# Attention's product with the values: values stationary and two query tiles moving, in place of probabilities stationary and values moving

## What is computed

```python
# q, k: (B, S, 4 heads, 2, 64); v: (B, S, 4 heads, 128)
scores = einsum("bqhmd,bkhmd->bhmqk", q * 64**-0.5, k)      # causal
p = softmax(scores, axis=-1)
a = p[:, :, 0] - lam * p[:, :, 1]
o = einsum("bhqk,bkhe->bqhe", a, v)                          # 128 dimensions per head
o = o * rsqrt(mean(o * o, axis=-1) + 1e-5) * subln_g * (1 - lam_init)
y_b = (o.reshape(b, s, 512) * silu(b_z)) @ w_b_out
```

## Time and profile before

| | us |
|---|---|
| median of 3 runs | 2308.67 (2306.83 to 2308.70) |
| the profiled execution | 2308.06 |
| its span, first to last instruction | 2306.3 |
| PE busy | 2278.6 (99%) |
| DVE busy | 1482.0 (64%) |
| ACT busy | 748.6 (32%) |
| POOL busy | 258.7 (11%) |

### The profile page before, as it was taken

How to read it: one execution, slowest core, us unless ns; L and a number is a source line. 1 busy time by engine, 2 the same in 40 slices (tenths; PEclk the granted TensorE clock), 3 DMA queues, 4 the chain that set the end, 5 groups by cost and what they waited for, 6 DMA issues and landing times.

```text
span 2306.3 us, 30415 instructions
## 1 busy us (share of the span) xinstructions
PE 2278.6 (99%) x11248; PEld 1860.0 (81%) x11248; DVE 1482.0 (64%) x3042; ACT 748.6 (32%) x1690; POOL 258.7 (11%) x250
## 2 busy tenths in 40 slices
PE   7999999999999999999999999999999999999998
PEld 6888888878888888888788888888878787888886
DVE  4787867773666665564567667665456666587752
ACT  4333332332333331121344344102135454441021
POOL 3455400100000000010000000001000000000010
PEclk9999999999999999999999999999999999999999
DMA  8877788887555545576644454556664444435555
GB/s 312 275 274 273 269 295 289 289 324 289 187 174 176 182 163 186 198 259 240 239 175 174 163 184 145 183 188 243 253 239 163 152 161 154 155 116 188 191 192 201
DMA packets 90610, 490.84 MB, mean 213 GB/s; under 512 B 9312, under 2 KB 9568, under 8 KB 45408
## 3 DMA queue, kind: packets, MB, share of 16 engines
q1 hardware_dynamic: 90464, 488.90, 59.6%
HBM read 375.61 MB, written 113.25 MB: 212 GB/s over the span
## 4 chain that ended last, share of the span: by engine, by line
PE 95%; DVE 2%; DMA 1%; ACT 1%; issue 1%; SPq 0%; DVEq 0%; ACTq 0%
PE PJ L637 73%; PE SC L696 6%; PE OB L758 5%; PE SC L728 5%; PE TB L737 3%; PE OB L696 1%; PE PJ L696 1%; DMA PX<-x_t 0%; PE TB L764 0%; DMA UC<-x 0%; PE TB L771 0%; DVE ZA L1253 0%; PE SC L637 0%; DVE Wp L1169 0%; PE OB L637 0%
## 5 line engine op out<-in xcount | busy, mean ns | idle before, releaser
L637 PE MATMUL PJ<-hT,Wp 128*128 128x512 f32 x6480 | 1575.6, 395 | 0.5 <-DVE PX L1448 0.5
L637 PEld LDWEIGHTS PJ<-hT,Wp 128*128 128x128 f32 x6480 | 1186.6, 188 | 254.1 <-issue 17.0
L1369 DVE SCALAR_TENSOR_TENSOR ACCS<-UA,col,ACCS 128x512 f32<-128x512 f32 x464 | 358.1, 812 | 0.1
L916 ACT ACTIVATE PX<-SC,negm 128x512 f32<-128x512 f32 (+3 forms) x320 | 196.3, 622 | 93.7 <-DVE negm L1208 73.1
L936 ACT ACTIVATE ZA<-TB 128x512 fp32r<-128x512 f32 (+3 forms) x160 | 85.6, 535 | 394.7 <-PE TB L737 394.6
L1253 DVE TENSOR_TENSOR ZA<-TB,ZA 128x512 fp32r<-128x512 f32 (+3 forms) x160 | 97.6, 610 | 178.4 <-ACT ZA L936 177.6
L1208 DVE TENSOR_REDUCE negm<-SC 128x2 f32<-128x1024 f32 (+3 forms) x160 | 169.2, 1060 | 35.3 <-PE SC L728 33.1
L970 ACT ACTIVATE TG<-PJ,col 128x512 f32<-128x512 f32 x64 | 44.1, 689 | 358.3 <-PE PJ L637 358.3
L758 PEld LDWEIGHTS OB<-VM,ZA 128*128 128x128 f32 x1088 | 145.4, 189 | 11.2
L758 PE MATMUL OB<-VM,ZA 128*128 128x128 f32 (+1 forms) x1088 | 154.1, 281 | 0.0
L696 PE MATMUL SC<-Wp,KM 128*128 128x512 f32 x384 | 121.4, 389 | 0.0
(11 more groups left out here) (172 smaller groups left out, 2016.0 us busy)
## 6 DMA issues: line engine op xcount, KB each, us to landing
Wp<-split_weights SPq DMA_DIRECT2D x264, 1024.0 KB, 4.8
split_weights<-Wp SPq DMA_DIRECT2D x88, 1024.0 KB, 4.9
Wraw<-w_stream SPq DMA_DIRECT2D x88, 512.0 KB, 5.8
KM<-keys SPq DMA_DIRECT2D x24, 512.0 KB, 4.5
VM<-values SPq DMA_DIRECT2D x24, 512.0 KB, 4.2
PX<-x SPq DMA_DIRECT2D x16, 512.0 KB, 6.8
out<-PX SPq DMA_DIRECT2D x16, 512.0 KB, 10.9
keys<-KM SPq DMA_DIRECT2D x12, 512.0 KB, 5.8
```

What stands on the lines that cost most here:

```text
L637: mm = pe.matmul(pj(c, r)[:, :], wt, rhs[:, 1 if q == 1 else 0, k, :], start=(n == 0), stop=(n == 3 * ktiles - 1))
L916: a = act.activation(PX[:, t % 2, j, m, 0:w], SC[k][:, m, 0:w], ACT.Exp, bias=negm[:, t % 2, j, m:m + 1], accum_out=lsum[:, t % 2, j, m:m ...
L1369: a = dve.scalar_tensor_tensor(out=acc, in0=src, scalar=col[:, n:n + 1], in1=acc, op0=ALU.mult, op1=ALU.add)
```

## The change

**Product with the values.** The values are stationary (v_hi and v_lo, 128x128 each), and the turned probabilities move, 256 columns wide: two query tiles 2q and 2q+1 side by side, a **pair** q. The output stands in `OB` with the head's dimensions on partitions and 256 queries in columns. A **turn** (q, j, g) takes two key blocks of a pair, that is four 128x128 transposes (three at the diagonal) into `TB`, and is followed by six products. There are 144 turns; all are 256 wide save three products in each of the 32 turns in which a block of one tile is masked away, which are 128 wide. The turns of a pair begin when its second tile is done, `TURN_GAP` steps apart (8, 6, 4, 3 for the four chunks).

**Norm.** The 32 pairs take the place of 64 tiles. ACT copies `OB` out (`o_copy`), DVE clamps a copy, ACT squares all of it, PE multiplies the squares by a 128x128 matrix of ones in float32 (`sum_squares`), so that the sum over dimensions stands in all partitions, 256 columns wide, and the power is raised on all of these. DVE then multiplies twice (`zb_pair`). `turn_o` is gone.

**Rooms.** The pieces of `PX` are given out by a table (`room_table`), first free first used, since a pair holds two tiles' probabilities for longer. In chunks 1 to 3 the norm's intermediates lie in `Wraw`, which only chunk 0 otherwise uses.

```diff
-                for b in range(nb):
-                    whole = (OB[:, 0:2 * P], AT[:, u % 2, 0, b, :], VM[:, blk, :])
-                    part = (OB[:, 0:P], AT[:, u % 2, 1, b, :], VM[:, blk, 0:P])
-                    for n, (dst, l, r) in enumerate((whole, part) if first else (part, whole)):
-                        mm = pe.matmul(dst, l, r, start=(first and n == 0), stop=(last and n == 1))
+                pe.matmul(dst, hi, AT[:, u % 2, 0, a0], start=first, stop=False)
+                pe.matmul(dst1, hi1, AT[:, u % 2, 0, a1], start=False, stop=False)
+                pe.matmul(dst1, hi1, AT[:, u % 2, 1, a1], start=False, stop=False)
+                pe.matmul(dst1, lo1, AT[:, u % 2, 0, a1], start=False, stop=False)
+                pe.matmul(dst, lo, AT[:, u % 2, 0, a0], start=False, stop=False)
+                pe.matmul(dst, hi, AT[:, u % 2, 1, a0], start=False, stop=last).then_inc(pv_done, 1)
...
-            def turn_o(c, h, t):
-                pe.wait_ge(on_ready, tile_at(c, h, t) + 1)
-                pe.transpose(TB[:, 0:P], o1[:, :], identf[:, :]).then_inc(ot_done, 1)
+            def sum_squares(c, h, q):
+                pe.wait_ge(osq_done, pair_at(c, h, q) + 1)
+                wait(pe, tb_free, TURN["o", c, h, q])
+                pe.matmul(TB[:, 0:2 * P], onesf[:, :], pair_rooms(c)[1], start=True, stop=True).then_inc(osum_done, 1)
...
-                pool.tensor_tensor(ost[:, 4, :], ost[:, 2, :], nhalf[:, 0:1], ALU.pow).then_inc(opow_done, 1)
+                pool.tensor_scalar(OV, OV, SUBLN_EPS, None, ALU.add).then_inc(oeps_done, 1)
+                pool.wait_ge(oeps_done, n + 1)
+                pool.tensor_tensor(OV, OV, nhalf[:, 0:1].to_broadcast([P, 2 * P]), ALU.pow).then_inc(opow_done, 1)
...
+                dve.tensor_scalar(OV, TB[:, 0:2 * P], FLT_MAX * OSCALE ** 2, 1.0 / (P * OSCALE ** 2),
+                                  ALU.min, ALU.mult).then_inc(ovar_ready, 1)
+                dve.scalar_tensor_tensor(out=OG, in0=TB[:, 0:2 * P], scalar=FLT_MAX * OSCALE ** 2, in1=SZB[:, k],
+                                         op0=ALU.is_le, op1=ALU.mult).then_inc(tb_free, 1)
+            def zb_pair(c, h, q):
                 dve.wait_ge(opow_done, n + 1)
+                wait(dve, zb_lo, n)
+                step(dve.scalar_tensor_tensor(out=ZF, in0=OT, scalar=col[:, COL_SG:COL_SG + 1], in1=OV,
+                                              op0=ALU.mult, op1=ALU.mult))
+                dve.wait_ge(tb_free, TURN["o", c, h, q] + 1)
+                dve.tensor_tensor(ZF, ZF, OG, ALU.mult).then_inc(zf_ready, 1)
```

More of the change, by code:

```diff
@@ L139, in loads_before, with pair_at, turns_in, turns_before @@
     return H * (c - 1 - j) + h
+def pair_at(c, h, q):
+    return 2 * (H * c + h) + q
+def turns_in(c):
+    return 4 * c + 3
+def turns_before(c):
+    return sum(H * turns_in(k) for k in range(c))
+def turned(c, h, q, j, g):
+    return turns_before(c) + h * turns_in(c) + q * (2 * c + 1) + 2 * j + g
+def turned_blocks(c, q, j, g):
+    return [(b, i) for b in (2 * g, 2 * g + 1) for i in range(2) if j < c or b <= 2 * q + i]
 def many_at(c, h, t):
     return 16 * (c - 1) + 4 * h + t
[L147 to L153, removed]
 def wdiff_at(c, h, t):
@@ L256, in tiles_at, with turned_table, turned_at, pairs_at @@
     return [(h, t) for h, t, j in units_at(c, p) if j == c]
+def turned_table(c):
+    table = {}
+    for h in range(H):
+        for q in range(2):
+            for j in range(c + 1):
+                for g in range(2 if j < c or q > 0 else 1):
+                    p = score_step(c, h, 2 * q + 1, c) + TURN_LAG[c] + TURN_GAP[c] * (2 * j + g)
+                    table.setdefault(p, []).append((h, q, j, g))
+    return table
+TURNED = [turned_table(c) for c in range(NCHUNK)]
+def turned_at(c, p):
+    return TURNED[c].get(p, ())
+def pairs_at(c, p):
+    return [(h, q) for h, q, j, g in turned_at(c, p) if j == c and g == q]
+SPARE = 13
+def room_table(c):
+    free = [(r, None) for r in range(SPARE if c == 0 else 4 * KB)]
+    room, last = {}, {}
+    for p in range(SPAN):
+        for j in range(c + 1):
+            for h, t in tiles_at(c, p - COMB_LAG[c] - j):
+                r = room[h, t, j, 1][0]
+                free.append((r, ("comb", unit(c, h, t, j) + 1)))
+                last[r] = p, free[-1][1]
+        for h, q, j, g in turned_at(c, p):
+            if g == 1 or (j == c and q == 0):
+                for i in range(2):
+                    r = room[h, 2 * q + i, j, 0][0]
+                    free.append((r, ("turn", turned(c, h, q, j, g) + 1)))
+                    last[r] = p, free[-1][1]
+        for h, t, j in units_of(c, p - EXP_LAG[c], 0) + units_of(c, p - EXP_ODD[c], 1):
+            for m in range(2):
+                room[h, t, j, m] = free.pop(0)
+    gates = sorted((last.get(r, (0, None)) + (r,) for r in range(2 * KB)), key=lambda x: (x[0], x[2]))
+    return room, [(r, done) for p, done, r in gates]
 HEAD_TAPS = (58, 46, 24, 0)
@@ L287, in tap_table @@
     return table
+ROOMS = [room_table(c) for c in range(NCHUNK)]
 TAPS = [tap_table(c) for c in range(NCHUNK)]
@@ L437, in build, with room, probs, room_free @@
         dve_step = sem("dve_step")
-        def gate_a(m):
-            return PX[:, 0, m % 4, 1 - m // 4, :]
+        def room(r):
+            return PX[:, r // (2 * KB), r // 2 % KB, r % 2, :]
+        def probs(c, h, t, j, m):
+            return room(ROOMS[c][0][h, t, j, m][0])
+        def room_free(eng, done):
+            if done is not None:
+                eng.wait_ge(comb_done if done[0] == "comb" else t_done, done[1])
+        def pair_rooms(c):
+            if c > 0:
+                return [Wraw[:, k // 4, k % 4 * 2 * P:(k % 4 + 1) * 2 * P] for k in range(5)]
+            return [room(SPARE + k // 2)[:, k % 2 * 2 * P:(k % 2 + 1) * 2 * P] for k in range(5)]
+        O2 = OB[:, 0:2 * P]
+        def gate_a(c, m):
+            return room(ROOMS[c][1][m][0])
         def merged(m):
@@ L1012, in _ @@
                 for p in range(SPAN):
-                    for u in units_at(c, p - HI_LAG[c]):
+                    for u in turned_at(c, p - HI_LAG[c]):
                         turned_hi(c, *u)
```

268 lines of the change are left out of this document (129 added, 139 removed).

## The result

| kernel | median, us | range | ratio to before (95% interval) |
|---|---|---|---|
| before (of the same chip) | 2308.68 | 2306.83 to 2308.75 | |
| changed | 3483.89 | 3483.03 to 3486.8 | 1.5096 (1.5069 to 1.5122) |

The account below looks back on a forecast made before the run. PE, 99% busy, was taken to bound the kernel. 2308 - 14 (PE's work) + 980 (waits of 28 pairs) + 127 (last pairs) + 58 (slow clock) = 3459, rounded to 3460 us; range 2285 to 3600.

Parts of the forecast that it names:

- the two ends given behind the sum: Whole kernel: about 3240 us with leads of 13 and no slow clock, 3650 with leads of 4.4 and twice the slow clock.
- PE's work, -14 us: On PE: value products -21.4 us, dropped output transposes -7.0, added float32 products with ones +14.4.
- part 2: DVE and ACT: both have less to do and neither bounds, so costed at nothing.
- The power, 40.3 us: POOL's power of 256 columns: 0.39 us plus 156 ns a column, a straight line from 1 and 4 columns.
- cheap power: Rival, 20%: POOL's power costs what a subtraction does, 0.86 us, and stays hidden; 2294 us, 2285 to 2308.
- in between: Rival, 18%: POOL's long powers cost less than the line, such as 40 ns a column for 2460 us; 2300 to 3240.
- Ready 41.2 us after `o_var`: In each pair's norm: 0.9 us until the epsilon is added, then the power, before the result is ready.
- DVE is held even earlier: DVE's `combine`, two SBUF inputs, cannot run beside POOL's power; were it otherwise, 6 us a pair or 180 us less.
- The lead of 8.5 and the catch-up of 2.2: PE runs on 8.5 us after `o_var` starts; DVE needs 2.2 after the power; 34.9 a pair, 980 for 28.
- The last pairs, 127 us: Each chunk's last pair, beside the gates: PE stops at the first `ZB` product, 34 us in three chunks, 25 in chunk 0.
- Slow clock, 58 us: PE runs slower after each idle stretch, at least 1.8 us lost, 32 times.
- The case against the forecast: Power short enough for PE's lead to hide: decided at 6.3 us in place of 41.2, below about 20 ns a column.

Follow-up runs that it names:

- e_pow2: Changed kernel with GpSimd's power raised on only 2 of the 256 columns, so most of the norm is left out: 2287.02 us, ratio 0.9905.
- e_beside_pow: `e_pow2` plus, 12 times in chunks 1 to 3, an unread GpSimd power of 160 columns running beside DVE: 2286.59 us, ratio 0.9904.
- e_sub2: `e_beside_pow` with 13 chained GpSimd subtractions of 768 columns in place of the unread power: 2327.25 us, ratio 1.0079.
- e_pow64: Changed kernel with GpSimd's power raised on 64 of the 256 columns: 2490.41 us, ratio 1.0787.
- e_diag2: Changed kernel with the power on 2 columns, its result put on diagonals by DVE and spread over partitions by PE: 2355.23 us, ratio 1.0199.

## Why the prediction came out right

Its direction and mechanism held; its close sum is partly luck. The range of 2285 to 3600 took in every rival, so that the time lies in it says little; what counts is the terms. By its own terms the two ends given behind the sum come to 3272 and 3629, not 3240 and 3650. Term by term:

- **PE's work, -14 us.** Measured -17 by the pieces and -19 by PE's busy time (`e_pow2`). A value product costs 0.12 (0.717 / 6), ones 0.441, a transpose of outputs 0.118, against 0.12, 0.45 and 0.11. The three came from the earlier trace rows. DVE and ACT cost nothing, as part 2 had it. The 1.8 us of slow clock that went away were not in the sum.
- **The power, 40.3 us.** Measured 41.15. The extrapolation by 64 times from 1 and 4 columns was 2% short. It hung on which row of one column was taken. That of the very power that is changed was left out of the earlier trace rows (kernel before, count, shortest/median/longest ns):

```profile
L1086 POOL TENSOR_TENSOR ost<-ost,nhalf x64: 543/636/1009, 64.7 to 2085.2; 128x1 f32<-128x1 f32 x64
```

With 636 in place of 550 the line would have given 127 ns a column and 33 us. Rival "cheap power" and "in between" fall: at 64 columns the slope is still 0.158 us.

- **Ready 41.2 us after `o_var`.** Measured 43.1 in the pair shown: 1.4 us to the power's start instead of 0.9, and there the power was 41.7.
- **"DVE is held even earlier".** This step failed. I had taken it from the earlier trace rows, where POOL's instruction was a subtraction, and carried it to the power. There were 180 us in it by the prediction's own count, and DVE's work behind the power took most of them back (next point). The trace shows the second of two combinations at 0.74 beside the power, and `e_beside_pow` shows it for 26 us. The rule that I had cited of the Trainium skill, page "SBUF — State Buffer", section "Who interferes with whom", holds for the subtractions of `e_sub2` and not for this power. The measurement decides.
- **The lead of 8.5 and the catch-up of 2.2.** Both were wrong in consequence. The first `turned_lo` gets through beside the power (1804.61), so PE has 13.5 us of work. Behind the power, `zb_pair` (0.9), two maxima (2.35), a tap (0.74) and the next `turned_lo` (0.69) then stand ahead of PE instead of two combinations: 5.0 us. The wait was to be 41.2 + 2.2 - 8.5 = 34.9 and is 43.1 + 5.0 - 13.5 = 34.6: a miss of 5.0 in the lead is made up by 1.9 in the power's end and 2.8 in the catch-up. Over the 28 pairs the idle time is 989 us, against 980. It isn't the same everywhere: 30 to 35 us in chunk 3, but 36.5 to 39 in chunk 0, where after a shorter lead PE stands at other copies, which free `PJ` and `TB` (waits, in total, times, longest):

```profile
PE PJ L726 <- DVE CT L1452: 152.6, 4, 38.9
...
PE TB L826 <- DVE VM L1403: 117.4, 3, 39.2
```

- **The last pairs, 127 us.** Measured 34.9, 31.9, 32.8 and 32.8, 132 in all. The 25 us for chunk 0 was 10 too small, the other three 1 to 2 each too large.
- **Slow clock, 58 us.** Measured 74. I took 1.8 us a wait from the one that the earlier trace rows shows; it is 2.3. The text said "at least that" without putting a number to it. This is the largest part of the miss: -5 of work, +14 of idle (9 of it in the 28 pairs, 5 in the last ones), +16 of clock, 25 us between the profiled execution and the sum.

The case against the forecast put the point where it turns at 20 ns a column, that is a power of some 5.4 us. By `e_pow64` a power of up to 6.6 us would be hidden in chunk 2, which is near it; but in chunk 0 only some 2 us would, some 6 ns a column, so that a power at 20 ns would not have been free.

## What to carry over

Before a small operation is made 256 times as wide because "the engine is idle", read its cost by the column from rows of two widths and carry it out to the new width. Here two rows, 550 and 1018 ns, told of 1200 us. Here the inverse root belonged on ScalarE, which was 33% busy: one of 256 columns takes 0.42 us and two table loads 2.6, and with it the new layout gains 0.65%, where GpSimd's power lost 51%. When a sum has a lead and a catch-up, check both by naming the instruction that PE really stops at, since one mistake on what may run beside a wait shifts both.

## What the runs showed of the hardware

- GpSimd's power costs 0.73 us on 2 columns, 10.55 on 64, 25.83 on 160 and 41.15 on 256, a line of 0.159 us a column, 75 times the 2.1 ns of its subtraction.
- It runs beside DVE instructions of two SBUF inputs without slowing them; GpSimd subtractions of 1.47 us stretch these from 0.74 to a median of 1.95 us where they overlap.
- Short idle stretches of PE cost nearly as much slow clock afterwards as those of 30 to 39 us: 57 us behind 28 of 2.2 to 8.6 us in `e_pow64`, 2.0 each (1.8 each behind the 17 of under 5 us), and 74 behind 32 in the changed kernel, 2.3 each. Not every one does: in `e_diag2`, behind two of three stretches of 2.7 us, the granted clock stayed at 1.00.
- DVE's reciprocal takes 1746 ns for 256 columns, 6.8 ns a column.
